# Expert products of three fixed token blocks issued over a whole PSUM bank instead of 256 columns each

## The reference, cut to what matters

```python
def swiglu(h, w_gu, w_down):
    g, u = jnp.split(h @ w_gu, 2, axis=-1)
    return (jax.nn.silu(g) * u) @ w_down

def moe_swiglu(h, w_router, w_gu, w_down):
    ...
    for e in range(N_EXPERTS):
        out = out + gates[:, e:e + 1].astype(t.dtype) * swiglu(t, w_gu[e], w_down[e])
```

## Time and profile before

| | before |
|---|---|
| median of 3 runs | 1482.8 us (1482.48 to 1485.57) |
| profiled execution, its own time | 1487.07 us |
| its span (first to last instruction) | 1485.3 us |
| instructions in the span | 44464 |
| mean granted TensorE clock | 0.984 |
| TensorE busy | 1421.9 us, 96% |
| HBM read | 476.95 MB, 325 GB/s over the span |

### The profile page before, as it was taken

One profiled execution on the slowest core, in us unless ns is written; L12 is line 12 of the kernel. 1 busy time (PEld: TensorE's weight loads), 2 busy tenths in 40 slices (PEclk: granted clock), 3 DMA queues, 4 the chain that ended last, 5 costly groups with the idle time before them and its releaser, 6 DMA issues.

```text
span 1485.3 us, 44464 instructions
## 1 busy us (share of the span) xinstructions
PE 1421.9 (96%) x21080; PEld 1019.0 (69%) x21081; DVE 428.7 (29%) x771; ACT 278.4 (19%) x476; POOL 30.1 (2%) x49
## 2 busy tenths in 40 slices
PE   8999999999988999999999999989989999998997
PEld 4887999999447866666666666665665666666665
DVE  6795998877667300000000000000000000000000
ACT  2562444443454200000000000001000000000000
POOL 1000000000000010000000000000000000000000
PEclk9999999999989999999999999999999999999999
DMA  9998489899531489999999999999999999998990
GB/s 354 355 370 298 158 284 340 284 340 343 224 114 62 193 315 344 361 356 379 402 356 373 402 366 362 401 372 364 401 374 373 383 391 353 387 402 340 379 390 17
DMA packets 172617, 485.09 MB, mean 327 GB/s; under 512 B 6160, under 2 KB 33008, under 8 KB 172432
## 3 DMA queue, kind: packets, MB, share of 16 engines
q1 hardware_dynamic: 168144, 474.04, 85.2%
q0 software_dynamic: 1680, 5.90, 1.7%
q10 hardware_dynamic: 2608, 2.27, 0.5%
HBM read 476.95 MB, written 5.24 MB: 325 GB/s over the span
## 4 chain that ended last, share of the span: by engine, by line
PE 94%; issue 2%; DVE 2%; ACT 1%; DMA 0%; ACTq 0%; POOL 0%; DVEq 0%
PE psum L1867 60%; PE psum L1653 5%; PE psum L1654 5%; PE psum L1655 5%; PE psum L1569 4%; PE psum L1465 3%; PE psum L1714 2%; PE psum L1548 2%; PE psum L1607 2%; PE psum L1533 1%; PE psum L1695 1%; PE psum L1509 1%; PE psum L1472 1%; PE psum L1517 1%; PE psum L1798 0%
## 5 line engine op out<-in xcount | busy, mean ns | idle before, releaser
L1867 PE MATMUL psum<-ring,xe 128*32 128x256 f32 (+1 forms) x12288 | 601.5, 354 | 24.6 <-issue 23.9
L1867 PEld LDWEIGHTS psum<-ring,xe 128*32 128x32 f32 x12288 | 387.5, 111 | 225.5 <-issue 33.8
L1389 DVE TENSOR_TENSOR hs<-sg,psum 128x768 f32<-128x768 f32 (+1 forms) x32 | 27.3, 854 | 866.8 <-PE psum L1867 866.8
L1867 PE MATMUL psum<-ring,hT 128*32 128x256 f32 x4608 | 263.7, 385 | 5.0 <-issue 5.0
L1867 PEld LDWEIGHTS psum<-ring,hT 128*32 128x32 f32 x4608 | 159.3, 112 | 100.0 <-issue 9.9
L1653 PE MATMUL psum<-fh,dhi 128*128 128x256 f32 x384 | 108.9, 283 | 3.7 <-DVE fl L1202 2.5
L1655 PE MATMUL psum<-fh,dlo 128*128 128x256 f32 x384 | 108.7, 283 | 0.0
L1654 PE MATMUL psum<-fl,dhi 128*128 128x256 f32 x384 | 108.7, 283 | 0.0
L921 ACT ACTIVATE hT<-psum 128x768 f32<-128x768 f32 x24 | 19.5, 810 | 427.6 <-PE psum L1465 427.6
L778 ACT ACTIVATE dhi<-ring 128x1024 fp32r<-128x1024 f32 x72 | 75.9, 1060 | 94.2 <-PE psum L1655 91.9
L1168 DVE TENSOR_TENSOR dlo<-ring,dhi 128x1024 fp32r<-128x1024 f32 x72 | 88.2, 1225 | 10.1 <-ACT dhi L778 7.9
(11 more groups left out here) (260 smaller groups left out, 1051.5 us busy)
## 6 DMA issues: line engine op xcount, KB each, us to landing
ring<-in_m_w_gu SPq DMA_DIRECT2D x112, 2048.0 KB, 13.1
ring<-in_m_w_down SPq DMA_DIRECT2D x56, 2048.0 KB, 12.8
ring<-in_ada_w SPq DMA_DIRECT2D x24, 2048.0 KB, 16.2
ring<-in_f_w_gu SPq DMA_DIRECT2D x24, 1024.0 KB, 13.1
ring<-in_f_w_down SPq DMA_DIRECT2D x6, 2048.0 KB, 14.8
ring<-in_a_w_in SPq DMA_DIRECT2D x4, 2048.0 KB, 20.0
ring<-in_kv_ada_w SPq DMA_DIRECT2D x4, 2048.0 KB, 9.3
ring<-in_a_w_out SPq DMA_DIRECT2D x2, 2048.0 KB, 15.6
```

What stands on the lines that cost most here:

```text
L1867: ins = mm(banks[TB * j:TB * j + TB, s * r:s * r + s], block(j, b), w[:, s * c:s * c + s], start=first and (s * r) % 512 == 0, stop=last, ...
```

## The change

`rounds` is reordered and its calls are made longer. It now walks over the 3s result columns in pieces of at most one PSUM bank (512 columns). For each piece, groups 0, 1 and 2 get one call each over the whole piece (slices 0 to 2 of the weights lie side by side, and each block stays the same), and then group 3 gets its calls of s columns, one for each block in the piece. For s = 256 the pieces are 512 and 256 columns wide, and a step is 3 + 2 + 3 + 1 = 9 calls. For s = 128 there is one piece of 384 columns, and a step is 3 + 3 = 6 calls. `start` clears a bank's accumulation flags for a group at its first product in each bank, as before. All that calls `rounds` is unchanged.

```diff
--- before.py
+++ after.py
@@ -1861,11 +1861,14 @@
 
             def rounds(banks, s, block, w, first, last):
 
-                for r in range(TBLKS):
-                    for j in range(TBLKS + 1):
-                        b, c = (j, r) if j < TBLKS else (r, TBLKS)
-                        ins = mm(banks[TB * j:TB * j + TB, s * r:s * r + s], block(j, b), w[:, s * c:s * c + s],
-                                 start=first and (s * r) % 512 == 0, stop=last, skip_group_check=True)
+                for c0 in range(0, TBLKS * s, 512):
+                    n = min(512, TBLKS * s - c0)
+                    for j in range(TBLKS):
+                        mm(banks[TB * j:TB * j + TB, c0:c0 + n], block(j, j), w[:, c0:c0 + n], start=first, stop=last,
+                           skip_group_check=True)
+                    for r in range(c0 // s, (c0 + n) // s):
+                        ins = mm(banks[TB * TBLKS:, s * r:s * r + s], block(TBLKS, r), w[:, TBLKS * s:TBLKS * s + s],
+                                 start=first and s * r == c0, stop=last, skip_group_check=True)
                 return ins
 
             def in_step(kind, b, t, h, i, w):
```

## The result

| | before | after |
|---|---|---|
| median | 1482.64 us (1482.04 to 1485.57) | 1443.18 us (1441.14 to 1444.46) |
| ratio of the two | | 0.9729, 95% interval 0.9711 to 0.9747 |
| profiled execution | 1487.07 us, span 1485.3 | 1444.03 us, span 1442.2 |
| instructions in the span | 44464 | 34096 |

The change makes the kernel 2.7% faster. 1442 us was forecast. Of the page after, here are the head, part 1, the code transfers of part 3, and the product groups of `rounds` in part 5 (line 1867 is the long call of groups 0 to 2, line 1870 the call of group 3). They answer to the earlier trace rows.

A forecast was written before the change was run, and what follows sets the result against it. TensorE bounds the kernel, stopping in last sets for code that takes 6.2 us a piece. Removing the stops and half clock saves 41.3 us, streaming and weight waits count nil: 1482.8 becomes 1441.5, said as 1442; range 1437 to 1456.

The forecast's parts named there:

- all 18 stops go, and with them the half clock that follows four: Expert stage: TensorE's 18 issue waits vanish, as do four 1.2 GHz spells after them; 41.3 us gained.
- Costing it by unit starts: Expert stage: gain taken from unit start times, not idle time; 37.1 us over six periods plus 4.2 in expert 0.
- The streaming price of nothing: Product steps in `rounds`: group 3's six records still set each step's length, so gain and loss are nil.
- Code supply: TensorE's instruction transfers: a piece lasts 7.0 us in the last set, 9.3 in wide stretches, over the 6.2 needed.
- each piece has to last by itself, with no store: Last sets: no stock of code builds up during slow wide stretches, so each piece must outlast 6.2 us.
- Rival 1: Weights run out in the last experts: some 7 us lost, 1449 us, or 1465 if 119.3 is the supply's pace; chance 0.12.
- Rival 2: Products end in program order, so group 3 lags 0.43 us some five times an expert: 17 us lost, 1459; chance 0.05.
- Rival 3: Column groups with unequal calls take turns: 0.43 us more on 608 steps, 260 us, 1700 us; chance 0.05.
- Rival 4: TensorE's stops are no matter of code supply and stay: 1482.8 us; chance 0.03.

The follow-up runs named there:

- e1: Changed kernel with the long calls only in each expert's last set, wide steps keeping 12 calls of 256 columns: 1444.31 us.
- e2: Changed kernel with the long calls only in the wide steps, the last set keeping its 12 calls of 128 columns: 1480.79 us.
- e5: Kernel before, with each weight transfer from the second expert on cut to its first row block, the rest stale: 1441.82 us.
- the two doses: Changed kernel, last set partly shortened: groups 0 to 2 get two calls for one of 384, 1446.29 us; up unit gets all old calls, 1453.49 us.
- nine calls: Changed kernel, but in the last set groups 0 to 2 get calls of 256 and 128 columns for one of 384: 1446.29 us.
- light weights: Changed kernel, with each weight transfer from the second expert on cut to its first row block, the rest stale: 1445.82 us.
- e3: Kernel before with the changed order but the old calls, each group getting all its calls of a bank in a row: 1494.84 us.

## Why the prediction was right

- **What the gain is.** The step "all 18 stops go, and with them the half clock that follows four" held: 0 stops, 41.3 us forecast. By the profiles 43.1 us went, 1.9 of them before the stage and by no doing of the change, so 41.2. By the medians it is 39.5 us, 1.8 less. The prediction had allowed up to 4 for that, since the runs without a profile lose a little less to the stops.
- **Costing it by unit starts** was the choice that made the size right. The idle time alone, 28.9 us, would have given 1454. Restarts and half clock were the other 12.
- **The streaming price of nothing.** 113.28 us a period without stops was worked out, 113.29 measured. Group 3, with its six records a step, sets the pace as before; groups 0 to 2 are 5 ns a step ahead of it, which they give back at the next transpose. e1 against the changed kernel shows the same as a total: 3648 products fewer, and the same 679.7 us.
- **Code supply.** A piece had to last over 6.2 us, and 7.0 us was enough. Shown by e1, e2, e5, the two doses and the code transfers that end before each restart. One sentence of this step was wrong: "each piece has to last by itself, with no store". There is a store, put at about 32 pairs in TensorE's queue, some 1.7 us for each last set. It didn't touch the sum, which was taken from measured starts, but it made the expectation for nine calls about four times too large. The sentence rests on a misread start. The last set of expert 4 doesn't begin 2 us ahead of its first stop but 4.8 us, with 96 products before the transposes (timeline of TensorE, kernel before):

```profile
1088.80 2.80 PE L1867 MATMUL psum<-ring,xe 128*32 128x128 f32 x96
```

The piece of code in use at 1093.62 was begun some 8 products into the set and lasted about 4.6 us, transposes included. Without a store a stop of about 1.6 us was due there. It was 0.23 us.
- **Rival 1, weights run out**: no. Landing took 11.3 to 15.0 us in the changed kernel between 985 and 1112 us, for 8.5 to 15.5, and light weights bring nothing. The supply of 389 GB/s was too low a bound: a window of the changed kernel reads 407, and the kernel before had 403 over 1042 to 1088 us.

```profile
1080.00:1092.00 12.00, 12.00 (x169) 1.00 1.02 407
```

- **Rival 2, ends in program order**: no. The 17 us that it priced aren't there: a period has 113.29 us, with no lag. In the timeline after, each of the three long calls leaves two records; their first ones start together at 1007.32 and their second ones at 1007.77, while group 3's first two, which stand behind all six in the program, start at 1007.34 and 1007.58. So the rule of the Trainium skill that was named there doesn't hold for the starts in different column groups. For the ends the profile has only modelled times.
- **Rival 3, unequal calls take turns**: no, the same rows. But its fear was near something real: e3 shows that an order can starve the groups, at six short records in a row for one of them.
- **Rival 4, another cause of the stops**: no, by e1, e5 and the code transfers.

## What to carry to other kernels

When an engine stops for "issue" at even counts of instructions, compare two times: how long it takes to use up a piece of code, and how long the next takes to come beside the data that the DMA engines carry. Only the stretch where the first is shorter loses anything, and there fewer, longer instructions gain all of it, however little they save elsewhere; cost it from the starts of units, since restarts and a fallen clock come on top of the idle time. And when calls for different column groups are reordered, keep the run of calls for one group short, or make the others' calls as long.

## What the runs showed of the hardware

- While weights stream at 378 GB/s, 256 instructions of TensorE take 6.2 us to come; the transfer itself is 1.1 us of it, and TensorE goes on some 1.4 us after its end. In the light kernel, at 101 GB/s, a piece used up in 3.5 us left almost no stop.
- Something ahead of the array covers the first 1.7 us or so of a shortage when a dense stretch follows a slow one; a queue of about 32 pairs of load and product fits the two doses to about 1 us (an estimate).
- Column groups run side by side at full pace with calls of unequal length (512 beside 2 x 256, 384 beside 3 x 128; 113.29 us a period). With 128-column calls in all groups, four records in a row for one group cost 0.3 us an expert at most; six in a row cost half as much time again (1 us for 0.66 a step).
- A stop of 2.5 us was followed by 3.4 us at 1.2 GHz in 4 of 8 cases (18 stops in all), so a short gap may cost 1.7 us more than itself. With no stops left, the clock stayed at 1.00 from expert 1 to the end.
